# Cumulated decays of the state-space heads as rows, spread by one 512-column product per four heads

## The reference, cut to what matters

```python
dt = softplus(dt + dt_bias);  a = -exp(a_log);  da = dt * a      # [chunk, 128, head]
acs = cumsum(da, axis=position)                                  # per chunk and head
seg = acs[l] - acs[s]
lmat = exp(where(l >= s, seg, -inf))                             # [head, l, s]
cb = einsum('ln,sn->ls', C, B)                                   # per chunk and group
y_diag = (cb * lmat) @ (dt * x)
states = B^T @ (exp(acs[-1] - acs) * dt * x)                     # end of chunk 0
y_off = exp(acs) * (C @ prev_states)                             # chunk 1 reads chunk 0's state
y = rms_norm((y_diag + y_off + d_skip * x) * silu(z))
```

## Time and profile before

| | |
|---|---|
| median of 3 runs | 958.75 us (957.27 to 959.83) |
| the profiled execution | 958.37 us, span 956.5 us |
| PE busy | 927.1 us, 97% of the span |
| VectorE busy | 680.6 us, 71% |
| ScalarE busy | 497.0 us, 52% |
| GpSimd busy | 56.4 us, 6% |

### The profile page before, as it was taken

How to read it: one execution, slowest core, us unless ns; L and a number is a source line. 1 busy time by engine, 2 the same in 40 slices (tenths; PEclk the granted TensorE clock), 3 DMA queues, 4 the chain that set the end, 5 groups by cost and what they waited for, 6 DMA issues and landing times.

```text
span 956.5 us, 13462 instructions
## 1 busy us (share of the span) xinstructions
PE 927.1 (97%) x5645; PEld 815.0 (85%) x5645; DVE 680.6 (71%) x784; ACT 497.0 (52%) x629; POOL 56.4 (6%) x79
## 2 busy tenths in 40 slices
PE   8999999999999999989999999999899999999997
PEld 7999878888888799976688888887899898888886
DVE  4976895897896865566758975668677866566664
ACT  5646854544636565666544545555354544444442
POOL 2025002000000000010010000000000000000000
PEclk9999999999999999999999999999999999999999
DMA  9743278899895462223579976655555455665531
GB/s 299 233 134 133 93 265 287 282 349 333 283 308 179 132 221 72 89 89 132 167 283 341 323 270 201 217 179 174 173 183 182 150 183 191 194 199 176 183 126 45
DMA packets 122756, 192.54 MB, mean 201 GB/s; under 512 B 6630, under 2 KB 103176, under 8 KB 119496
## 3 DMA queue, kind: packets, MB, share of 16 engines
q1 hardware_dynamic: 116496, 157.00, 50.2%
q0 software_dynamic: 5824, 33.90, 9.7%
q10 hardware_dynamic: 376, 0.78, 0.2%
HBM read 190.60 MB, written 1.06 MB: 200 GB/s over the span
## 4 chain that ended last, share of the span: by engine, by line
PE 71%; DVE 8%; ACT 4%; issue 2%; DVEq 0%
PE PS L663 19%; PE PS L664 10%; PE PS L615 9%; PE PS L617 9%; PE PS L616 9%; PE PS L608 3%; PE PS L610 3%; PE PS L609 3%; DVE lo L1698 3%; ACT hi L1230 1%; DVE stats L1784 1%; PE PS L736 1%; DVE r L1777 1%; DVE x_tok L1797 1%; ACT hid L1559 1%
## 5 line engine op out<-in xcount | busy, mean ns | idle before, releaser
L1698 DVE TENSOR_TENSOR lo<-raw,hi 128x2048 fp32r<-128x2048 f32 (+1 forms) x147 | 329.5, 2264 | 94.3 <-ACT hi L1230 94.2
L663 PE MATMUL PS<-x_both,hi 128*128 128x512 f32 x848 | 297.0, 393 | 0.0
L1230 ACT ACTIVATE hi<-raw 128x2048 fp32r<-128x2048 f32 (+1 forms) x147 | 271.7, 1885 | 9.1 <-DMA raw<-even_w_in 5.1
L664 PE MATMUL PS<-x_both,lo 128*128 128x256 f32 x848 | 237.5, 280 | 0.0
L663 PEld LDWEIGHTS PS<-x_both,hi 128*128 128x128 f32 x848 | 159.0, 187 | 35.7
L664 PEld LDWEIGHTS PS<-x_both,lo 128*128 128x128 f32 x848 | 159.9, 189 | 1.3
L615 PE MATMUL PS<-hi,hid_hi 128*128 128x512 f32 x352 | 139.3, 396 | 0.5 <-DVE hid_lo L1997 0.5
L617 PE MATMUL PS<-hi,hid_lo 128*128 128x512 f32 x352 | 138.9, 394 | 0.0
L616 PE MATMUL PS<-lo,hid_hi 128*128 128x512 f32 x352 | 138.8, 394 | 0.0
L608 PE MATMUL PS<-x_both,hi 128*128 128x256 f32 (+1 forms) x472 | 135.0, 286 | 3.0 <-DVE lo L1698 1.7
L609 PE MATMUL PS<-x_both,hi 128*128 128x256 f32 (+1 forms) x472 | 133.3, 282 | 0.0
(11 more groups left out here) (302 smaller groups left out, 1002.7 us busy)
## 6 DMA issues: line engine op xcount, KB each, us to landing
raw<-ffn_w_gate SPq DMA_DIRECT2D x22, 1024.0 KB, 7.8
raw<-ffn_w_up SPq DMA_DIRECT2D x22, 1024.0 KB, 6.3
raw<-ffn_w_down SPq DMA_DIRECT2D x22, 1024.0 KB, 5.1
raw<-mlp_w_in SPq DMA_DIRECT2D x16, 1024.0 KB, 5.3
raw<-mlp_w_out SPq DMA_DIRECT2D x16, 1024.0 KB, 5.0
sq<-ada_w POOLq DMA_DIRECT2D x12, 1024.0 KB, 7.1
r<-ada_w POOLq DMA_DIRECT2D x12, 1024.0 KB, 5.9
raw<-sc_w_in SPq DMA_DIRECT2D x12, 1024.0 KB, 5.2
```

Of the source, the lines that this page charges most:

```text
L663: pe.matmul(PS[:, bank + m, :], wh, x_both[:, :, k, :], start=k == 0, stop=False, skip_group_check=True)
L664: last = pe.matmul(PS[:, bank + m, 0:S], wl, x_hi[:, k, :], start=False, stop=k == KT - 1, skip_group_check=True)
L1230: act.activation(split_view("hi", c), split_view("raw", c), ACT.Copy).then_inc(hi_split, 1)
L1698: dve.tensor_tensor(split_view("lo", c), split_view("raw", c), split_view("hi", c).bitcast(F32), ALU.subtract).then_inc(lo_split, 1)
```

## The change

It replaces the 16 f32 products of each `bcast` by 4 F32R products of 512 columns, and makes their operands.

- VectorE, at the start: `of_half`, [128, 2, 128], ones in partitions 0 to 63 for chunk 0 and in 64 to 127 for chunk 1.
- VectorE, in `small`: `steps4`, the da columns of `tok` repeated four times for each chunk, and `of_head`, [128, 16], which is 1 where the row belongs to head h (a sum of four slices of the identity). `cb` is copied after them.
- TensorE, in `head` 0: two f32 products, one for each chunk, with `steps4` (64 columns) stationary and `triu` moving. They write the cumulated sums as rows, head by head, into partitions 0 to 127 of bank 0; each head has four equal rows per chunk.
- VectorE, in `head` 0, after `decay` and ahead of `x_dt`: a rounded copy of these rows (`acs_rows`), the remainders of rows 32 to 63 and 96 to 127, and four products of 128 x 512 into `by_row` ([128, 16, 128]), a block diagonal in which a row stands only under its own head. Both chunks are served by this one `by_row`.
- TensorE, in `bcast`: four products, `of_half` of the chunk stationary, four heads of `by_row` moving. In chunk 0 product q waits for quarter q of `by_row`.
- The buffers of the convolution give their place to `by_row`, which waits for its last reader.

```diff
+            by_row = sb("by_row", [P, HEADS, P], F32R, even)
...
+                    pe.wait_ge(sem("tok_ready"), 2)
+                    for c in range(2):
+                        last = pe.matmul(PS[64 * c:64 * c + 64, 0, P:2 * P], steps4[:, c, :, :].rearrange("p r c -> p (r c)"), triu,
+                                         start=True, stop=True, skip_group_check=True)
+                    last.then_inc(sem("acs_done"), 1)
...
-                for h in range(HEADS):
-                    last = pe.matmul(PS[:, h // 4, (h % 4) * P:(h % 4) * P + P],
-                                     tok[:, j, 16 + h:17 + h].to_broadcast([P, P]), triu, start=True, stop=True)
-                    if h % 4 == 3:
-                        last.then_inc(sem("acs_bcast"), 1)
+                for q in range(4):
+                    if j == 0:
+                        pe.wait_ge(sem("acs_ready"), 3 + q)
+                    pe.matmul(PS[:, q, :], of_half[:, j, :], by_row[:, 4 * q:4 * q + 4, :], start=True, stop=True)\
+                      .then_inc(sem("acs_bcast"), 1)
...
+                dve.wait_ge(sem("tok_ready"), 1)
+                for j in range(2):
+                    ins = dve.tensor_copy(steps4[:, j, :, :], tok[:, j, 16:32].rearrange("p (o c) -> p o c", o=1)
+                                          .to_broadcast([P, 4, 16]))
+                ins.then_inc(sem("tok_ready"), 1)
+                dve.wait_ge(sem("ident_landed"), 16)
+                link(dve.tensor_tensor(of_head[:, :], ident[:, 0:16], ident[:, 32:48], ALU.add))
+                link(dve.tensor_tensor(of_head[:, :], of_head[:, :], ident[:, 64:80], ALU.add))
+                dve.tensor_tensor(of_head[:, :], of_head[:, :], ident[:, 96:112], ALU.add)
...
+                    link(dve.tensor_copy(acs_rows[:, :], PS[:, 0, P:2 * P]))
+                    for rs in (slice(32, 64), slice(96, 128)):
+                        ins = dve.tensor_tensor(acs_rows[rs, :], PS[rs, 0, P:2 * P], acs_rows[rs, :].bitcast(F32), ALU.subtract)
+                    link(ins)
+                    dve.wait_ge(sem("xbc_ready"), 6)
+                    for q in range(4):
+                        four = slice(4 * q, 4 * q + 4)
+                        dve.tensor_tensor(by_row[:, four, :], acs_rows[:, :].bitcast(F32).rearrange("p (o n) -> p o n", o=1)
+                                          .to_broadcast([P, 4, P]), of_head[:, four].rearrange("p (h o) -> p h o", o=1)
+                                          .to_broadcast([P, 4, P]), ALU.mult).then_inc(sem("acs_ready"), 1)
```

More of the change, by code:

```diff
@@ L128, in build @@
             z_silu = sb("z_silu", [P, KT, S], F32, even)
-            conv_in = sb("conv_in", [P, 2, 2, 3 + S], F32, even)
-            conv_acc = sb("conv_acc", [P, 2, 2, S], F32, even)
+            with ExitStack() as even_conv:
+                conv_in = sb("conv_in", [P, 2, 2, 3 + S], F32, even_conv)
+                conv_acc = sb("conv_acc", [P, 2, 2, S], F32, even_conv)
+            by_row = sb("by_row", [P, HEADS, P], F32R, even)
+            sb("conv_rest", [P, 16], F32, even)
             xbc = sb("xbc", [P, 12, S], F32, even)
             tok = sb("tok", [P, 2, 32], F32, even)
+            steps4 = sb("steps4", [P, 2, 4, 16], F32, even)
+            acs_rows = sb("acs_rows", [P, P], F32R, even)
+            of_half = sb("of_half", [P, 2, P], F32R, even)
+            of_head = sb("of_head", [P, HEADS], F32, even)
             neg_acs = sb("neg_acs", [P, 2, 16], F32, even)
@@ L879, in even_head @@
                         pe.matmul(PS[:, 0, 64 + 16 * c:80 + 16 * c], triu, tok[:, c, 16:32], start=True, stop=True)
-                    pe.matmul(PS[:, 0, 96:112], ones[:, :], tok[:, 0, 16:32], start=True, stop=True)\
-                        .then_inc(sem("acs_done"), 1)
+                    pe.matmul(PS[:, 0, 96:112], ones[:, :], tok[:, 0, 16:32], start=True, stop=True)
+                    pe.wait_ge(sem("tok_ready"), 2)
[3 more added lines that the diff above has]
+                    last.then_inc(sem("acs_done"), 1)
                 if j == 0:
@@ L1915, in _ @@
             dve.memset(ones_r[:, :].bitcast(F32), 1.0)
+            link(dve.memset(of_half[:, :, :].bitcast(F32), 0.0))
+            for j in range(2):
+                dve.memset(of_half[64 * j:64 * j + 64, j, :].bitcast(F32), 1.0)
             dve.memset(eps_sb[:, 0:1], LN_EPS)
```

## The result

The change makes the kernel slower. Six runs give a median of 967.68 us (967.0 to 970.18), six runs of the kernel before beside them 959.29 us (957.27 to 960.53): a ratio of 1.0088, 95% interval 1.0072 to 1.0104, or +8.4 us. The forecast of 962.1 had the direction, but 967.68 lies outside its range of 959.8 to 964.2. The profiled execution took 967.6 us with a span of 965.8 us.

A forecast was written before the change was run, and what follows sets the result against it. Chunk 0 was taken as bound by VectorE's list through ScalarE to TensorE: `y` 0 1.90 us later plus 1.5 of slow clock, 3.4 on 958.37, gives 961.8; the median lies 0.38 above, hence 962.1 us, range 959.8 to 964.2.

The forecast's parts named there:

- TensorE's busy share is no guide: Mixer, 51 to 103 us: TensorE is busy 50.4 of 52.0 us, yet that poorly shows what its work is worth.
- VectorE's list bounds chunk 0: Chunk 0: the chain VectorE, ScalarE, TensorE is bound by VectorE's list, with 1.38 us to spare before `y` 0.
- The releaser of `y` 0: TensorE before `y` 0: the gap of about 4 us would be released by ScalarE's `state`.
- the place of both waits and the size of the second: TensorE would stand idle 4.0 us ahead of `y` 0 and about 2.9 us ahead of `pool` 1.
- The price of the new products on TensorE: Four F32R products take 0.95 us per `bcast`, the two from `steps4` 0.35; TensorE has 4.8 us less to do.
- the five small rows ahead of the copy of `cb`: VectorE in `small`: together 1.0 us, costing nothing because the split behind waits 2.04 us for ScalarE.
- the later stages take up nothing: Behind the mixer, nothing has slack to absorb a delay, so what comes out late stays late.
- the term of 3.23 us: VectorE's new rows in `head` 0, ahead of `x_dt`: everything behind them starts 3.23 us later, 3.1 to 3.9.
- The clock, first stretch: Behind the idle time before `y` 0, TensorE's clock halves on the path, costing 1.5 us (1.1 to 1.7).
- one stretch is one sample: Argument for the rival that `y` 0 comes 1.90 us late but the clock holds: 960.65 us, 30 in 100.
- The clock, second stretch: The 2.9 us idle ahead of `pool` 1, broken by work, were expected to cost nothing in clock.
- The rival called dearer: VectorE's rows at 3.9 us (+2.57) and the clock also falling ahead of `pool` 1: 964.3 us, 12 in 100.

The follow-up runs named there:

- experiment 4: Kernel before with four 512-column products per `bcast` on data already there, without VectorE's new instructions and the `steps4` products; 959.29 us, ratio 0.9998.
- experiment 5: Changed kernel with the old f32 products back in `bcast`; `by_row` is made but not read; 966.16 us, ratio 1.0073.
- experiment 1: Changed kernel plus unread products of ones in TensorE's two empty stretches, 24 ahead of `y` 0 and 12 ahead of `pool` 1; 964.25 us, ratio 1.0048.
- experiment 2: Changed kernel with GpSimd's window sums held back until VectorE has done the split behind `x_dec`; 964.8 us, ratio 1.004.
- experiment 3: Changed kernel with unread products (17 ahead of `y` 0, 12 ahead of `pool` 1) and GpSimd's window sums held back; 961.81 us, ratio 1.0033.
- run 8: Kernel before with chunk 1's steps reordered as in run 7, and `by_row` made during `state` 0 and read only by `bcast` 1; 961.16 us, ratio 1.0014.
- experiment 6: Changed kernel with `bcast` 0 in its old f32 form and the rows made during `state` 0, read only by `bcast` 1; 962.05 us, ratio 1.0034.
- run 9: Run 8 with one VectorE split and `x_dt` moved between the masked sums, and ScalarE's scaling of `pool` 0 ahead of its split; 958.18 us, ratio 0.9995.
- run 7: Kernel before, only reordered: `bcast` 1 directly behind `y` 0, both pool steps behind `proj` 12 with banks of their own; 961.34 us, ratio 1.0004.

## Why the prediction was wrong

**Right.** That TensorE's busy share is no guide, and that VectorE's list bounds chunk 0 with 1.38 us to spare (experiments 4 and 5). The releaser of `y` 0, the place of both waits and the size of the second. The price of the new products on TensorE. That the five small rows ahead of the copy of `cb` cost nothing: the split behind them still waited 1.20 us. That a low clock stands behind `y` 0's wait, on the path (experiment 1). That the later stages take up nothing.

**The step that failed** is the term of 3.23 us, with the sentence that everything behind these rows on VectorE starts that much later. It was priced as if VectorE ran alone. The rows themselves took 3.48. But moving `x_dec` and the split later also moved them beneath GpSimd's window sums, 1.82 us more (experiment 2). The prediction looked at GpSimd only as one who might be slowed beside a busier VectorE, and at its last difference, not at its first sum at 65.62, which had just lost to the split. With 5.57 in place of 3.23, 0.27 of it the start of the column products, `y` 0 is 4.33 late and not 1.90. The other kernels start those products anywhere from 56.34 to 57.80 us, so the 0.27 can't be laid to the change. (The 0.05 taken from the state copies to `y` 0 was 0.15.) This term alone carries the sum out of its range: with 4.33 in place of 1.90 and the clock as forecast it gives 964.6. The other way round, with 1.90 and the measured price of the clock (3.58), it gives 964.2, the range's end.

The rule for this is in the Trainium skill, page "SBUF — State Buffer", section "Who interferes with whom": a VectorE instruction with two SBUF inputs contends with a GpSimd instruction that reads SBUF, and the one that issues first decides who blocks. The traces agree: before, the split was first and GpSimd's sum took 3.36 us; after, GpSimd was first and the split took 3.55. `x_dt` and the masked sums, which read PSUM and one SBUF operand, kept 1.29 and 0.68 beside the same sums.

**The clock, first stretch.** Taken at 1.5 us from one stretch of 3.6 us, it cost 2.41. TensorE does the same work from `y` 0 to `head` 1 in before, after and experiments 1 to 5, and takes 7.76 us for it before and in experiment 1, where the clock is 1.00. After it took 10.17 behind 5.98 us of idling; in experiment 2 9.32 behind 4.17; in experiment 5 10.33 behind 3.53. So the price, 2.41, 1.56 and 2.57 us, didn't follow the length of the wait: the shortest of the three was the dearest. In after and in experiment 5 the clock fell during the wait and stayed at 0.50 until about 91.0 and 90.2 us. In experiment 2 it fell when `y` 0 had already started, and was back at 1.00 from 88.5. One stretch was too few to price this term, and its stated 1.1 to 1.7 too narrow. Nor is that stretch the same in every execution: of the eleven traced kernels, which all run this code of the second layer, before, experiments 1, 3 and 4 and run 8 show the low clock behind its waits of 1.53 and 1.63 us, and the other six, after among them, don't. The doubt that "one stretch is one sample" was right, though `y` 0's much longer wait brought the low clock in all three traces that have it (after, experiments 2 and 5).

**The clock, second stretch.** It was put at nothing, being shorter than the stretch that fell and broken by 1.1 us of work. It cost 1.17. The clock fell with 2.79 us in experiments 2 and 4 too, with 2.99 in 6 and with 2.63 in run 8, and held behind 1.66 (run 9) and 1.69 (run 7). These two don't show that a wait of this size is safe: behind one wait of 1.78 to 1.79 us that every kernel has in its second layer (331.24 before, 339.35 after), the clock fell in after, in experiment 2 and in run 7, and held in the other eight. The rival called dearer had this term and a costlier VectorE for another reason, with 12 in 100; its 964.3 is still 3.4 us short.

The sum, as it should have stood: 0.27 + 3.48 + 1.82 - 1.23 + 2.41 + 1.17 = 7.9, measured 7.91 at `y` 1 and 8.4 in the medians. The terms are read from the same trace as the 7.91, so that they meet it proves nothing; what shows them are experiment 2 (the 1.82), experiment 1 (the two of the clock) and experiment 3 (the rest).

**Open.** Why the low clock lasted for 5.1 us of work in after and 5.3 in experiment 5, but for some 3 us in the earlier trace rows and in experiment 2, isn't settled, and with one trace of each kernel it isn't known whether other executions do the same. Whether run 9 owes its clock to the shorter wait or to chance isn't shown either. Nor is it known why the output took 1.1 us longer to write in the profiled execution.

## What to carry to other kernels

Where TensorE waits for another engine's chain, products taken off it are worth the slack of that chain and no more; here 1.2 us, though TensorE was 97% busy. Work added to the bounding engine costs its own length and whatever its successors now collide with: when a list is shifted in time, lay it against the other engines' rows anew and see what comes to run beside what. Time won in front of a wait is idle time, and the waits of 2.8 to 6.0 us here cost another 1.2 to 2.6 behind them, so a kernel can gain by doing useless products there. One trace is thin evidence on the clock: before a term is priced by it, look at the same unchanged wait in the traces of several kernels.

## What the runs showed of the hardware

- The same wait of 1.78 to 1.79 us, in code that no kernel changed, was followed by the low clock in three of eleven traces, and the pair of 1.53 and 1.63 us in five of eleven.
- Ones-products that nobody reads made the kernel 3.4 us quicker (967.68 to 964.25).
- Behind 5.98 us of empty TensorE the granted clock was 0.50 for 5.13 us of work; behind 2.79 us it fell too (0.50 from 108.40 to 111.50), though work (`pool` 1, from 107.41) had begun again by then.
- The slow stretch behind `y` 0's wait cost 2.57 us after 3.53 us of idling, 1.56 after 4.17 and 2.41 after 5.98.
- GpSimd's sums stretched VectorE's 128 x 2048 split from 2.28 to 3.55 us and its 128 x 1024 product from 1.23 to 1.78; four 128 x 512 products with both operands in SBUF took 3.18 us beside GpSimd and 2.50 without.
- Three linked VectorE sums of 16 columns start 0.20 us apart; a remainder on 32 partitions takes 0.30.
